# Seven block products for the down projection, and weight sums moved from DMA to VectorE, in a float32 decoder layer

## The reference

```python
h = rms_norm(x, norm_ffn[i])
f_gate, f_up = jnp.split(h @ w_gate_up[i], 2, axis=-1)
x = x + (jax.nn.silu(f_gate) * f_up) @ w_down[i]
ple_gate = jax.nn.sigmoid(rms_norm(x, ple_norm[i]) @ w_ple_gate[i])
x = x + ple_gate * (p[i] @ w_ple_proj[i])
```

## Time and profile before

| | before |
|---|---|
| median of 3 runs | 1759.92 us (1759.28 to 1760.42) |
| the profiled execution, its own time | 1760.17 us |
| its span, first to last instruction | 1758.5 us |
| PE busy | 1745.5 us, 99% |
| DVE busy | 1201.5 us, 68% |
| ACT busy | 897.3 us, 51% |
| granted TensorE clock, mean | 0.999 |

### The profile page before, as it was taken

How to read it: one execution, slowest core, us unless ns; L and a number is a source line. 1 busy time by engine, 2 the same in 40 slices (tenths; PEclk the granted TensorE clock), 3 DMA queues, 4 the chain that set the end, 5 groups by cost and what they waited for, 6 DMA issues and landing times.

```text
span 1758.5 us, 24598 instructions
## 1 busy us (share of the span) xinstructions
PE 1745.5 (99%) x8924; PEld 1471.6 (84%) x8924; DVE 1201.5 (68%) x1406; ACT 897.3 (51%) x993; POOL 246.9 (14%) x367
## 2 busy tenths in 40 slices
PE   9999999999999999999999999999999999999998
PEld 7888888889888888888888888888888888888887
DVE  7698897988867545454666777775457777665666
ACT  6764464555555443444445555554335555544555
POOL 5026071450710000000011000000000000000021
PEclk9999999999999999999999999999999999999999
DMA  7566565564657656666568777746687777566664
GB/s 275 171 189 180 156 195 178 143 208 137 199 173 222 192 189 192 192 182 199 180 187 275 228 231 230 236 145 191 193 273 228 232 234 228 159 182 195 187 210 133
DMA packets 108324, 348.53 MB, mean 198 GB/s; under 512 B 23680, under 2 KB 24080, under 8 KB 107984
## 3 DMA queue, kind: packets, MB, share of 16 engines
q1 hardware_dynamic: 89888, 325.36, 59.2%
q0 software_dynamic: 3968, 16.52, 4.3%
q10 hardware_dynamic: 14384, 5.52, 1.3%
HBM read 333.71 MB, written 3.16 MB: 192 GB/s over the span
## 4 chain that ended last, share of the span: by engine, by line
PE 87%; issue 4%; POOL 4%; ACT 1%; DVE 1%; DMA 1%; ACTq 0%; POOLq 0%; DVEq 0%; SPq 0%
PE acc L426 44%; PE acc L432 22%; PE acc L405 7%; PE acc L410 3%; PE ps L1057 2%; POOL blk_x L623 2%; POOL blk_t L621 2%; PE acc L1057 2%; PE ps L1060 1%; PE acc L1060 1%; PE ps L1029 1%; ACT whi L384 0%; PE acc L1041 0%; PE acc L1040 0%; PE acc L1039 0%
## 5 line engine op out<-in xcount | busy, mean ns | idle before, releaser
L398 DVE TENSOR_TENSOR wlo<-raw,whi 128x1024 fp32r<-128x1024 f32 x564 | 712.8, 1269 | 487.2 <-ACT whi L384 477.6
L384 ACT ACTIVATE whi<-raw 128x1024 fp32r<-128x1024 f32 x563 | 593.6, 1058 | 661.6 <-PE acc L432 521.2
L426 PE MATMUL acc<-whi,ax 128*128 128x512 f32 x2176 | 539.6, 390 | 0.8 <-ACT whi L1230 0.8
L426 PEld LDWEIGHTS acc<-whi,ax 128*128 128x128 f32 x2176 | 407.0, 188 | 85.7 <-issue 1.8
L432 PE MATMUL acc<-wlo,ax 128*128 128x512 f32 x1088 | 291.0, 389 | 0.0
L432 PEld LDWEIGHTS acc<-wlo,ax 128*128 128x128 f32 x1088 | 204.2, 188 | 42.8 <-DVE wlo L398 0.4
L405 PE MATMUL acc<-ax,whi 128*128 128x512 f32 x896 | 228.7, 397 | 0.1
L405 PEld LDWEIGHTS acc<-ax,whi 128*128 128x128 f32 x896 | 160.9, 189 | 30.4 <-ACTq L1388 0.3
L426 PE MATMUL acc<-whi,fx 128*128 128x512 f32 x704 | 174.4, 390 | 0.0
L426 PEld LDWEIGHTS acc<-whi,fx 128*128 128x128 f32 x704 | 131.8, 188 | 27.2
L410 PEld LDWEIGHTS acc<-ax,wlo 128*128 128x128 f32 x896 | 122.1, 190 | 9.1
(11 more groups left out here) (315 smaller groups left out, 1598.3 us busy)
## 6 DMA issues: line engine op xcount, KB each, us to landing
raw<-in_win SPq DMA_DIRECT2D x223, 512.0 KB, 4.1
raw<-in_wgu SPq DMA_DIRECT2D x136, 512.0 KB, 4.3
raw<-in_wd SPq DMA_DIRECT2D x88, 512.0 KB, 4.0
unit<-in_wgu SPq DMA_DIRECT2D x50, 512.0 KB, 4.9
raw<-in_wb SPq DMA_DIRECT2D x32, 512.0 KB, 4.2
raw<-in_wo SPq DMA_DIRECT2D x32, 512.0 KB, 4.2
raw<-in_wpg SPq DMA_DIRECT2D x32, 512.0 KB, 4.2
unit<-unit POOLq DMA_DIRECT2D x20, 512.0 KB, 7.6
```

The lines of the kernel that those rows point to most:

```text
L384: nc.scalar.activation(whi[:, s], raw[:, src], ACT.Copy).then_inc(hi_done, 1)
L398: nc.vector.tensor_tensor(wlo[:, s], src, whi[:, s].bitcast(F32), ALU.subtract).then_inc(lo_done, 1)
L426: nc.tensor.matmul(into[buf][:, m], x[:, WIDE_K * h + kt, q, m * P:(m + 1) * P], whi_w[:, s, kt], start=(m in first if isinstance(first, t ...
```

## The change

It does four things.

1. **Down projection in pairs.** Column blocks 0 and 1 of `down_a` become the pair `down_a0`, blocks 2 and 3 the pair `down_a1`, blocks 0 and 1 of `down_b` the pair `down_b0`. In each, the first eight K tiles go through two units of seven products. Blocks 2 and 3 of `down_b` stay plain (`down_b1`). So there are 16 units in place of 10.
2. **All weight sums on DVE.** The accumulating DMAs go, and the second load of B12. `sum_t3`, `sum_t1`, `sum_t2`, `sum_t4` are four DVE additions per unit, in six buffers in place of eight.
3. **An order table.** `PAIRS` has a string for each pair: `f` is a product slot, `0` and `1` are plain halves of the first and the second column block. A gate and up pair's order changes too: products at 0, 2, 4, 6, 8, 10, 11 (before: 0, 2, ..., 12).
4. **Sums of activations six times** instead of once (`sum_inputs`, `sums_high`, `sums_low`; events 0 to 5), into two buffers `sx`, and the small load of `p` with its split moves from the DeltaNet stage to `down_b1`.

The core of the diff:

```diff
+UNIT_FORMS = (B11, T1, B21, B22, T3, T2, T4)
+FFN_ORDER = "f0f0f0f0f0ff0111111"
+PAIRS = {**{f"ffn{i}": FFN_ORDER for i in range(1, PART_A)},
+         "down_a0": "0000f0f0f0f0f1f1f1f1ff1ff1ff11", "down_a1": "f0f0f0f0f0f0f0f0f1f1f1f1f1f111",
+         **{f"ffn{i}": FFN_ORDER for i in range(PART_A, PART_A + PART_B)},
+         "down_b0": "0000f0f0ff1f1f1ff1fff1fff1"}
...
-            for k in range(FB // 2 - 1):
-                pool.wait_ge(unit_in[0], 48 * (k + 1))
-                pool.dma_start(unit[T1][:], unit[B11][:], accum_op=ALU.add).then_inc(t_added, 16)
-                pool.wait_ge(unit_in[1], 32 * (k + 1))
-                pool.dma_start(unit[T3][:], unit[B22][:], accum_op=ALU.add).then_inc(t_added, 16)
...
+            def pair(name, after={}, free_from=None):
+                for n in range(PER[name]):
+                    h = H0[name] + n
+                    if h in PLAIN:
+                        block, c = PLAIN[h]
+                        if c == 0 and block == 0:
+                            acc_free(pe, name, 0, 0, 0)
...
+                    else:
+                        if h == PLACE[PAIR_UNITS[name][0]][B11]:
+                            pe.wait_ge(ps_free, free_from)
+                            j = PAIR_NAMES.index(name)
+                            if j:
+                                pe.wait_ge(u_made, U_BASE[PAIR_NAMES[j - 1]] + 4)
+                        form(name, h)
+                    if n in after:
+                        after[n]()
...
-            for b in range(MB):
-                down_block("down_a", b, 2 * PART_A,
-                           {} if b else {3: lambda: turn_f(PART_A - 1), 2 * PART_A - 3: operand_ready(ff_lo, PART_A)})
+            pair("down_a0", {2: lambda: turn_f(PART_A - 1), 19: operand_ready(ff_lo, PART_A)}, f_turned(PART_A))
+            pair("down_a1", {}, f_turned(PART_A))
...
+            pair("down_b0", {2: lambda: turn_f(FB // 2 - 1), 3: operand_ready(ff_lo, FB // 2)}, f_turned(FB // 2))
+            gemm("down_b1", 0, 0, 2 * PART_B, 0, 0, fx, rows=True, after={1: lambda: turn_x(1, 0), 4: lambda: turn_x(1, 1)})
...
+            pair("down_a0", {3: (turned_high(PART_A - 1),), 9: (sums_high(2, 0, PLACE[PAIR_UNITS["ffn5"][0]][T2]),),
+                             21: (copy_p1("down_a0", PART_A),)})
...
+            def add_sums(name, half, sums, b):
+                def stage():
+                    dve.wait_ge(u_made, U_BASE[name] + 4 + half)
+                    x = xtok[:, :, WIDE * b:WIDE * (b + 1)]
+                    v.tensor_tensor(x, x, sums, ALU.add).then_inc(u_made, 1)
...
+                stages = {0: before[0], 1: before[1], 3: (sum_t4(k),), 11: (lower_sums(name, up_sum[i], i - 1),), 12: (upper_sums(name, up_sum[i]),),
+                          13: (gate_add(i),), 14: (sum_t3(k + 1),), 15: (turned_low(i - 1),) if turned else (), 16: (sum_t1(k + 1),), 18: (sum_t2(k + 1),)}
...
+            pair("down_a0", {0: (up_add(5),), 1: (product(5),), 4: (turned_low(5),), 6: (sum_t4(k),), 7: (sum_inputs(fx, 4, 2),), 9: (sums_low(2, 0),),
+                             11: (sum_t3(k + 1),), 13: (sum_t1(k + 1),), 17: (sum_t2(k + 1),), 19: (sum_t4(k + 1),), 25: (sum_t3(k + 2),),
+                             26: (sum_t1(k + 2),),
+                             27: (lower_sums("down_a0", down_up, PART_A),), 28: (upper_sums("down_a0", down_up),),
+                             29: (add_sums("down_a0", 0, gate_sum, 0), add_pair("down_a0", 0, 0, MB + 1), sum_t2(k + 2))})
+            pair("down_a1", {0: (add_sums("down_a0", 1, down_up, 1),), 1: (add_pair("down_a0", 1, 1, MB + 2),),
+                             3: (sum_t4(k + 2),), 7: (sum_t3(k + 3),), 10: (sum_t1(k + 3),), 13: (sum_t2(k + 3),), 17: (sum_t4(k + 3),),
+                             21: (sum_t3(k + 4),), 24: (sum_t1(k + 4),),
+                             25: (lower_sums("down_a1", down_up, PART_A), sum_inputs(ax, 0, 3)), 26: (upper_sums("down_a1", down_up),),
+                             27: (add_sums("down_a1", 0, gate_sum, 2), sums_low(3, 0)),
+                             28: (add_pair("down_a1", 0, 2, MB + 3), sum_t2(k + 4)), 29: (add_sums("down_a1", 1, down_up, 3),)})
...
+            pair("down_b0", {0: (up_add(10),), 1: (product(10),), 4: (turned_low(10),), 6: (sum_t4(k),), 7: (sum_inputs(fx, 4, 5),), 9: (sums_low(5, 0),),
+                             10: (sum_t3(k + 1),), 12: (sum_t1(k + 1),), 15: (sum_t2(k + 1),), 17: (sum_t4(k + 1),),
+                             24: (lower_sums("down_b0", down_up, FB // 2), upper_sums("down_b0", down_up)),
+                             25: (add_sums("down_b0", 0, gate_sum, 0), add_pair("down_b0", 0, 0, 2 * MB + 1))})
```

More of the change, by code:

```diff
@@ L560, in _ @@
+            for name in PAIR_NAMES:
+                load_pair(name)
+            for n in range(PER["down_b1"]):
+                load_plain(H0["down_b1"] + n, wd, ((2 + n // (2 * PART_B)) * HFFW + 2 * PART_A + n % (2 * PART_B)) * P)
             for n in range(PER["proj"]):
@@ new lines, in copy_p1, with stage, silu_sum @@
+            def copy_p1(name, products):
+                def stage():
+                    act.wait_ge(half_used, PLACE[PAIR_UNITS[name][-1]][B11] + 1)
+                    act.wait_ge(ff_prod, products)
+                    j = PAIR_NAMES.index(name)
+                    if j:
+                        act.wait_ge(u_made, U_BASE[name])
+                    f(gate_sum[:, 0], ps[0][:, 0], ACT.Copy).then_inc(p1_copied, 1)
+                return stage
+            def silu_sum(i):
+                def stage():
+                    act.wait_ge(sum_full, 2 * i - 1)
+                    gate_silu(i, gate_sum)
+                return stage
@@ new lines, in turned_high, with pair, ffn @@
+            def turned_high(i):
+                return lambda: f_high(i)
+            def pair(name, stages):
+                for n in range(PER[name]):
+                    split_hi(act, name, 0, n)
+                    for stage in stages.get(n, ()):
+                        stage()
+            def ffn(i, turned, extra={}):
+                pair(f"ffn{i}", {3: (copy_p1(f"ffn{i}", i),), 14: ((turned_high(i - 1),) if turned else ()) + (silu_sum(i),), **extra})
+            ffn(1, True)
+            ffn(2, True)
@@ new lines, in _ @@
+            ffn(9, True)
+            ffn(10, True)
+            pair("down_b0", {3: (turned_high(FB // 2 - 1),), 9: (sums_high(5, 0, PLACE[PAIR_UNITS["ffn10"][0]][T2]),),
+                             19: (copy_p1("down_b0", FB // 2),)})
+            for n in range(PER["down_b1"]):
+                split_hi(act, "down_b1", 0, n)
+                if n == 2:
+                    x_high(1, 0, C_PLE)
+                if n == 5:
+                    x_high(1, 1, C_PLE)
+                if n == 8:
+                    act.wait_ge(p_in, 16)
+                    f(phi, praw[:], ACT.Copy).then_inc(p_hi, 1)
+                if n == 2 * PART_B + 2:
+                    x_high(1, 2, C_PLE)
@@ L2194, in _ @@
-            ffn({0: (lambda: x_low(0, MB - 1, C_FFN),), 5: (lambda: mean_columns(0),), 7: (sum_inputs,), 9: (sums_low,)})
-            for it in range(PART_A - 1):
-                seven("ffn_a", it, it, True, it < PART_A - 2)
-            def finish_f(k):
-                return {0: (lambda: up_add(k),), 1: (lambda: product(k),), 4: (lambda: f_low(k + 1),)}
-            last = finish_f(PART_A - 2)
-            for b in range(MB):
-                for n in range(2 * PART_A):
-                    split_lo(dve, "down_a", 0, b * 2 * PART_A + n)
-                    for stage in last.get(n, ()) if b == 0 else ():
-                        stage()
-                    if b == MB - 1 and 9 <= n < 11:
-                        weight_sum(PART_A - 1, *SUMS[n - 9])
-                acc_full(dve, "down_a", 0, (b + 1) * 2 * PART_A)
-                x = xtok[:, :, WIDE * b:WIDE * (b + 1)]
-                v.tensor_tensor(x, acc[b % 2][:], x, ALU.add).then_inc(res[1]["x"], 1)
-                dve.wait_ge(res[1]["x"], b + 1)
-                dve.sem_inc(acc_read[b % 2], 1)
@@ new lines, in sum_t2, with stage @@
+            def sum_t2(k):
+                def stage():
+                    dve.wait_ge(t1_added, k + 1)
+                    if k:
+                        dve.wait_ge(t4_added, k)
+                        dve.wait_ge(lo_done, PLACE[k - 1][T2] + 1)
+                    v.tensor_tensor(unit[T2][:], unit[T1][:], unit[B22][:], ALU.add).then_inc(t_made, 1)
+                return stage
+            for n in range(2 * HWIDE):
+                split_lo(dve, "ffn0", 0, n)
+                if n == 0:
+                    x_low(0, MB - 1, C_FFN)
+                if n == 5:
+                    mean_columns(0)
+                if n == 7:
+                    sum_inputs(ax, 0, 0)()
+                if n == 9:
+                    sums_low(0, 0)()
+                if n == 11:
+                    sum_t3(0)()
+                if n == 13:
+                    sum_t1(0)()
+                if n == 15:
```

(17 more changed lines are left out.)

617 lines of the change are left out of this document (323 added, 294 removed).

## The result

| | before | changed |
|---|---|---|
| median, us | 1759.68 (1759.28 to 1760.42, 4 runs) | 1777.22 (1776.27 to 1778.88, 4 runs) |
| profiled execution: own time, span, us | 1760.17, 1758.5 | 1777.48, 1775.9 |
| mean granted clock over the span | 0.999 | 0.994 |
| PE matmuls | 8924 | 8888 |

The ratio is 1.0100, with a 95% interval of 1.0083 to 1.0118: 17.5 us slower. The forecast was 1770 and slower; the sign was right, the size was 7.2 us short, and the time lies just above the range of 1765 to 1777.

The account below looks back on a forecast made before the run. PE was taken as the bound, busy for 99% of the span. -8.16 us of matmuls, +17.7 of waits and +0.5 of restarts gave +10.0 us, a median of about 1770, range 1765 to 1777.

Parts of the forecast that it names:

- -8.16 us for 36 matmuls: PE, six more units: each replaces four plain halves by seven products, saving 1.36 us, -8.16 us in all.
- Sums, loads and the moved `p` at nothing: Beside PE: added DVE weight sums, fewer loads, and `p` moved under plain slots of down_b1 cost nothing.
- The places and sizes of the waits: Handovers of ps[0] and acc[0] in the down projection: PE waits in five places, 17.7 us in all.
- (b): End of down_b0: DVE frees acc[0] only after sums and additions, so PE stands for 4.8 us.
- +0.5 for the start of PE after the stalls: PE's restart after each of the five stalls, taken at 0.1 us each: +0.5 us.
- (c): End of down_a0: acc[0] is freed late, so PE waits 2.7 us at slot 1 of down_a1.
- a rival with 12%: PE's clock drops in a stall, 2.7 to 5.4 us each; one or two drops give 1773 to 1780; chance 12%.
- (a): Starts of down_a0 and down_b0: PE waits for ps[0] after turn_f, 3.85 us each, +7.7 us.
- (d): End of down_a1: acc[0] is freed late, behind sum_inputs and other sums, so PE waits 2.5 us.
- The clock falls in the stage: Feed-forward stage: the clock was to stay at 1.00; a fall there would show the prediction wrong.
- The covered handovers: Rival: DVE empties buffers in its slack, so the waits shrink; down to 1752 us with none; chance 7%.

Follow-up runs that it names:

- the sums alone: Kernel before, with all four weight sums of a unit on DVE and no accumulating DMA, ten units kept: 1759.31 us, ratio 0.9998.
- the waits alone: Kernel before, with only the change's first handover in down_a and down_b, so PE waits for ps[0]; all matmuls kept: 1770.94 us, ratio 1.0067.

## Why the prediction was right and wrong

- **-8.16 us for 36 matmuls: right.** It came out as 8.2 us of PE's busy time once the waits were gone; the time fell by 7.0 (4.4 to 9.1 by the interval).
- **Sums, loads and the moved `p` at nothing: right.** DVE at 32.56 of 42 in pair 1 (forecast 33.1), no wait of PE in a gate and up pair, and the sums alone gave a ratio of 0.9998.
- **The places and sizes of the waits: right.** 17.5 measured, 17.7 forecast, none off by more than 0.07. The chain of place (b), counted from the start of slot 24 (1599.22), had `lower_sums` at 2.50, the addition of `gate_sum` at 6.27, that of `acc[0]` at 7.52; measured 2.49, 6.28, 7.53. `sum_inputs` was estimated at 3.0 and took 3.11.

  ```profile
  1601.71 0.68 DVE L2284 TENSOR_TENSOR t<-ps,t 128x512 f32<-128x512 f32 x1
  ...
  1605.50 1.22 DVE L2315 TENSOR_TENSOR xT<-xT,t 128x1024 f32<-128x1024 f32 x1
  1606.75 1.22 DVE L2135 TENSOR_TENSOR xT<-acc,xT 128x1024 f32<-128x1024 f32 x1
  ```

- **+0.5 for the start of PE after the stalls: the step that failed.** It should have been +7.9 here. Where the clock stayed up, 0.13 was right (the half behind (c): 2.85). Where it fell, the cost behind a wait was 1.55 to 2.76. The text had this case as a rival with 12%, and argued it down: it read in the earlier trace rows that the clock is full for 4 to 5 us after PE's last matmul (5.1 by these rows), so waits of 3.85 and 4.8 would be too short. That took one delay, seen once, at the end of a program, for the least delay there is. In the nine traces this same delay is anything from 2.3 to 5.1 us. In that of the waits alone, PE's last matmul ends at 1761.17, and this is the clock:

  ```profile
  1763.00:1764.00 1.00, 0.00 (x0) 0.00 (x0) 0.66 (x5) 0.67 (x3) 0.00 (x0) 0.73 0.00 0
  ```

  At the first place (a) the clock fell less than 3 us after PE had stopped, and at (d) after 2.28 us of idle time, within 2 us of new work. "The clock falls in the stage" was one of the prediction's own signs of being wrong.
- **The rival's size was wrong too:** it counted "one or two" drops at 2.7 to 5.4 each. There were four drops of five waits at 1.55 to 2.76. The plain halves behind (b) and (d) took 4.44 and 4.03, not twice 2.72, since the clock was low for only a part of them; at both (a) a part of the low clock fell into the wait, where it costs nothing. That 1777.2 lies in the rival's 1773 to 1780 comes from more drops than it counted, at less each.
- The prediction cited the Trainium skill's page "TensorE: Matmul & The Clock Gate", Part 1, on windows that run free of the program, so that a stall may or may not meet one. The traces agree with that "may or may not": over the six traces that have waits of 1.9 to 2.3 us at the ends of `down_a0` and `down_a1` or one of 3.6 to 4.6 us elsewhere, the clock fell at 4 of 10 of the short and at 11 of 11 of the long ones. By these counts, which the prediction did not have, the drop is a term of the sum and not a rival: for the three long waits in full, for the two short ones at a little under half.
- **The covered handovers (7%, 1752):** they weren't covered, but 1752 is where the kernel lands when they are.

## What to carry to other kernels

Where one engine is the bound and always busy, read a change of order from the buffers: for every handover, take the start of the last slot that feeds the emptying operation, add up what stands ahead of that operation on its own engine, and compare with when the bound engine is back. Put the operation that frees a buffer ahead of work that frees nothing; here that turned +17.5 us into -7. And when TensorE must stand, add the half clock behind the wait to the sum, on top of the wait itself: 1.5 to 2.8 us each time that it came, which was all 11 times behind waits of 3.6 to 4.6 us and 4 of 10 times behind waits of 1.9 to 2.3 us.
